# Order of low-weight and high-weight matmuls inside the up projections of two feed-forward layers

## The reference

```
def squared_relu_mlp(hn, w_up, w_down):                       # twice, w_up 1024 x 4096
    return jnp.square(jax.nn.relu(hn @ w_up)) @ w_down
...
hf = _rms_norm(x, norm_ffn_pre[l])                            # once, w_up 1024 x 5632
u = _dwconv_causal(hf @ w_up[l], ffn_dw[l]) + ffn_dw_b[l]
u_g, u_v = jnp.split(u, 2, axis=-1)
yff = (jax.nn.silu(u_g) * u_v) @ w_down[l]
```

## Time and profile before

| | |
|---|---|
| median of 3 runs | 1251.53 us (1250.41 to 1251.58) |
| profiled execution | 1249.54 us |
| its span, first to last instruction | 1247.8 us |
| mean granted TensorE clock | 0.998 |
| PE busy | 1217.6 us, 98% of the span |
| weight loads (PEld) busy | 1095.9 us, 88% |
| DVE busy | 872.1 us, 70% |
| ACT busy | 699.9 us, 56% |
| mean HBM traffic | 168 GB/s |

### The profile page before, as it was taken

One profiled execution on the slowest core, in us unless ns is written; L12 is line 12 of the kernel. 1 busy time (PEld: TensorE's weight loads), 2 busy tenths in 40 slices (PEclk: granted clock), 3 DMA queues, 4 the chain that ended last, 5 costly groups with the idle time before them and its releaser, 6 DMA issues.

```text
span 1247.8 us, 21521 instructions
## 1 busy us (share of the span) xinstructions
PE 1217.6 (98%) x8583; PEld 1095.9 (88%) x8583; DVE 872.1 (70%) x1252; ACT 699.9 (56%) x1016; POOL 58.4 (5%) x102
## 2 busy tenths in 40 slices
PE   8999989999999999999999999999999999999997
PEld 7999978888888998888888999999999977888886
DVE  5898467566666656666656579999656577778876
ACT  5984565555455554555554664666453456666663
POOL 5020020000000001000000000000000010000000
PEclk9999999999999999999999999999999999999999
DMA  7771134666554644465555566354546634566551
GB/s 224 195 203 70 36 126 148 222 207 206 177 186 147 216 164 142 171 204 180 177 193 169 169 203 186 121 161 150 183 148 202 196 108 136 185 199 196 189 193 68
DMA packets 160340, 210.80 MB, mean 169 GB/s; under 512 B 5542, under 2 KB 143220, under 8 KB 160261
## 3 DMA queue, kind: packets, MB, share of 16 engines
q1 hardware_dynamic: 157315, 202.77, 50.9%
q0 software_dynamic: 1904, 6.85, 1.4%
q10 hardware_dynamic: 1042, 0.07, 0.1%
HBM read 208.62 MB, written 1.05 MB: 168 GB/s over the span
## 4 chain that ended last, share of the span: by engine, by line
PE 77%; DVE 11%; ACT 5%; issue 3%; DMA 2%; SPq 1%; POOL 1%; DVEq 0%; POOLq 0%; ACTq 0%
PE bank L372 16%; PE bank L376 16%; PE bank L375 15%; PE bank L457 15%; PE bank L453 7%; DVE wlo L308 4%; ACT whi L300 2%; PE bank L1428 2%; DVE common L2585 1%; DMA raw<-in_dn_w_in 1%; PE bank L1448 1%; ACT common L756 1%; SPq L3391 1%; PE bank L2006 1%; PE bank L2098 1%
## 5 line engine op out<-in xcount | busy, mean ns | idle before, releaser
L308 DVE TENSOR_TENSOR wlo<-raw,whi 128x2048 fp32r<-128x2048 f32 x190 | 434.7, 2290 | 197.8 <-ACT whi L300 197.5
L300 ACT ACTIVATE whi<-raw 128x2048 fp32r<-128x2048 f32 x190 | 363.1, 1912 | 144.5 <-PE bank L372 43.1
L372 PE MATMUL bank<-xparts,whi 128*128 128x256 f32 x912 | 259.7, 285 | 0.4 <-DVE common L2767 0.4
L376 PE MATMUL bank<-xparts,wlo 128*128 128x256 f32 x912 | 255.5, 280 | 0.0
L375 PE MATMUL bank<-xparts,whi 128*128 128x256 f32 x912 | 253.6, 278 | 0.0
L457 PE MATMUL bank<-xparts,whi 128*128 128x512 f32 x832 | 209.2, 393 | 0.0
L372 PEld LDWEIGHTS bank<-xparts,whi 128*128 128x128 f32 x912 | 171.2, 188 | 2.8 <-issue 2.2
L457 PEld LDWEIGHTS bank<-xparts,whi 128*128 128x128 f32 x832 | 148.7, 188 | 27.4
L375 PEld LDWEIGHTS bank<-xparts,whi 128*128 128x128 f32 x912 | 171.5, 188 | 0.7 <-issue 0.5
L376 PEld LDWEIGHTS bank<-xparts,wlo 128*128 128x128 f32 x912 | 171.3, 188 | 0.0
L372 PE MATMUL bank<-whi,hhi 128*128 128x512 f32 x392 | 155.2, 396 | 3.7 <-DVE hlo L1064 1.9
(11 more groups left out here) (391 smaller groups left out, 1679.0 us busy)
## 6 DMA issues: line engine op xcount, KB each, us to landing
raw<-in_mlp_w_up SPq DMA_DIRECT2D x32, 1024.0 KB, 5.5
raw<-in_mlp_w_down SPq DMA_DIRECT2D x32, 1024.0 KB, 5.1
raw<-in_w_in SPq DMA_DIRECT2D x22, 1024.0 KB, 5.2
raw<-in_w_up SPq DMA_DIRECT2D x22, 1024.0 KB, 5.1
raw<-in_w_gate SPq DMA_DIRECT2D x16, 1024.0 KB, 5.5
raw<-in_dn_w_in SPq DMA_DIRECT2D x15, 1024.0 KB, 5.9
raw<-in_mb_w_in SPq DMA_DIRECT2D x12, 1024.0 KB, 5.2
raw<-in_w_down SPq DMA_DIRECT2D x11, 1024.0 KB, 4.9
```

Of the source, the lines that this page charges most:

```text
L300: nc.scalar.activation(whi[:, s, :], raw[:, r, :], ACT.Copy).then_inc(hi_ready, 1)
L308: nc.vector.tensor_tensor(wlo[:, s, :], raw[:, V % RAW, :], f32(whi[:, s, :]), ALU.subtract).then_inc(lo_ready, 1)
L372: ins = pe.matmul(o, shi, mhi, start=first, stop=False, skip_group_check=True)
L376: return pe.matmul(o, slo, mhi, start=False, stop=last, skip_group_check=True)
```

## The change

In the second branch of `wide_features` the second loop over k is taken away, so that the high product of a k follows its low product at once. The matmuls, their operands, their banks, the waits ahead of them and the semaphores that they raise stay the same; only their order inside a feature tile differs.

More of the change, by code:

```diff
@@ L486, in wide_features @@
                             ins.then_inc(unit_begun, 1)
-                    for k in range(KT):
                         ins = high_weights(f, k, k == KT - 1)
```

## The result

The changed kernel is slower by a little: 1255.89 us (median of 6 runs, 1254.85 to 1258.73) against 1251.28 us for the kernel before (6 runs), a ratio of 1.0042 with a 95% interval of 1.0032 to 1.0052 (the ratio is estimated over all runs; the two medians alone give 1.0037). I had forecast no change, 1251.5 us. The time lies inside the range, near its upper end, but outside the 1249.0 to 1254.0 us that I gave to the forecast itself: it went the way of the rival that I called "slower: the long cadence wins". The profiled execution took 1254.85 us with a span of 1253.1 us, 5.3 us longer than before; the clock is the same, 0.998.

A forecast was written before the change was run, and what follows sets the result against it. TensorE's steps, without gaps, were taken to bound the up-unit stages. 800 pairs x 0 ns added 0 us to the median of 1251.5 us, so the forecast was 1251.5 us, with a range of 1247.5 to 1256.4 us.

The forecast's parts named there:

- slower: the long cadence wins: Rival, chance 0.21: in pairs, low steps of 120.0 ns, +3.0 us; with high steps of 236 ns, +6.7 us.
- What bounds the kernel: In up-unit stages time is the sum of TensorE's steps; PE busy all 144.57 us of the first loop.
- The count: 50 up units of 16 pairs move, 800 low and high pairs; 1 ns on a pair is 0.8 us.
- no wait, no idle time: No wait comes or goes in the up units, put at zero; the loop's window should show no idle time.
- What a changed neighbour costs: Inside a tile, changing weights or width costs nothing visible; pairs stay at 116 + 231 ns, 800 x 0 = 0.
- The choice among the bounds: For a pair between 334 and 360 ns, -11 to +10 us, it took the middle, 347.5 ns.
- the short cadence: Low steps of 113.8 ns, as in the second tile; as faster rival, pairs of 340 ns, -6.0 us, chance 0.19.
- its two prices of 231 and 236: High steps in the slower rival's pairs: 231 ns gives +3.0 us in all, 236 ns +6.7 us; chance 0.21.
- my sign for it: In the changed kernel's timeline, an up unit of 5.61 us or more would mean the long cadence.
- What stands before and after a tile meets the same neighbour: At tile ends, still low product first and high product last, so signals come at the same place; put at zero.
- Weight loads two ahead: Low products' loads hiding under high ones: low step 109.2 ns, about -5.7 us; not used in the forecast.

The follow-up runs named there:

- the probe of entries: TensorE-only kernel, equal blocks behind entries of differing width: 256-column steps settled at averages of 118.7, 116.7 or 113.3 ns, pairs at 346.7 or 360.0 ns.
- groups of two: Against the changed kernel, two low products then two high ones through the tile: one run, 1250.50 us beside 1250.12 for before.
- eight and eight at place 0: Kernel before, order kept, with both halves of xparts moved to a multiple of 16 numbers: 1259.14 us, 1.0062 of before.

## Why the prediction was wrong

- *What bounds the kernel* was right. TensorE steps without a gap before and after, and the 4.8 us that the steps grew by are in the span.
- *The count* of 800 pairs was right, and so was *no wait, no idle time*. The loop's window shows none.
- *What a changed neighbour costs* is the step that failed. I read two joins, found them as long as the steps in their blocks, and put the pair at the average of before, 347.5 ns, with 800 x 0 as the sum. A join of before is entered from a settled block and shows one step out of it. It doesn't show the cadence that a run of joins settles into. That is 353 ns here, and the average over an up unit is 351.6 (5.626 / 16 us), 352.5 in the convolutional layer. In place of 0, the 800 pairs cost 3.4 us (2.1 in the low steps, 1.35 in the high ones).
- *The choice among the bounds* was the weak point in it. The rows showed that the same product steps at 113.8 or 118.8 ns, and I took the mean of both, as if a block kept half of its luck. I also took the entries of the two tiles for the same; to the ns they are 236 and 231, and the probe of entries showed that what enters a block can pick its cadence. The low products of the second tile lost the short cadence for good: they average 119.0 now, close to the rival's 120.0; the high ones 233.2, between its two prices of 231 and 236. The direction was that of the slower rival, to which I gave 0.21, and so was the mechanism in the pairs; my sign for it, a unit of 5.61 us or more, is what came. Its price, 3.0 to 6.7 us, holds the pairs' 3.4 and the 4.6 measured, but the down units' 1.35 wasn't in it, and that the whole still fits is luck. That the time lies inside my range is owed to the part of this rival that I took into the range, not to the sum.
- *"What stands before and after a tile meets the same neighbour"*, and so no term for the down units, failed too. The neighbour is the same instruction, but it doesn't hand over in the same time: the last high product ahead of a down unit steps in 227 ns (242.13 to 242.35 above), where it took 236. The untouched 512-column products of the down units hold 238, 231, 231 ns in place of steps that averaged 231.7, 0.041 us a unit and 1.35 us in all, over a quarter of the loss. It depends on the place of the weights that they load: with the hidden tiles at (16, 16) it is gone in the loop.
- *Weight loads two ahead* have no support: pairs would have become faster. In the changed kernel, as before, nearly every load of a low or high product starts 1 to 4 ns after the start of the matmul just ahead of its own.
- What stays open is what in TensorE makes the steps settle. The runs show three things that it depends on (the entry, the order, and the place of an operand in its tile, of the moving one in the probes and of the loaded weights with the hidden tiles) and four that it doesn't depend on here (whether the low product's weights are in `wlo` or `whi`, the half of the bank, other engines, and for 512 columns the width of the load). They don't show the mechanism; that the moment of handing over carries the pattern on fits all of them, but was argued and not measured.

## What to carry to other kernels

Where TensorE runs without gaps, a reordering that keeps every instruction can still move the time by some tenths of a per cent, in either direction (0.4% slower at the kernel's place of `xparts`, some 0.3% faster at the other), and can move it in code behind it that wasn't touched. Don't take the average of an irregular step for the step of a new order: copy the loop's matmuls, with their places in memory, into a kernel that does nothing else, and read the settled steps there; here that gave the loop's units to the nanosecond as long as the tiles had the kernel's sizes too; the convolutional layer, with another order of units, did not follow that copy at (16, 16). Tune order and operand placing together, and compare whole turns of the loop, not the block that was edited.

## What the runs showed that I had not expected

A settled step of an fp32r product took from 112 to 124 ns for 256 columns and from 225 to 241 ns for 512, at a granted clock of 1.00, and repeated in patterns of two to eight steps, or of two turns of a loop (up units of 5.533 and 5.595 us), for as long as the order lasted. Shifting an operand by 12 numbers changed the time of units that don't read it.

The lengths of the settled patterns have a common measure. Averaged over ten turns or more, the loop's turns take 11120.0 ns (before), 11133.4 (groups of two), 11226.6 (changed), 11240.0 (eight and eight at place 0), and 11053.3 and 11146.7 (hidden tiles at (16, 16), eight and eight and then pairs). To within 0.1 ns these are 1668, 1670, 1684, 1686, 1658 and 1672 times 6.667 ns. The pairs of the entry probe, 346.7 and 360.0 ns, are 52 and 54 times that. So a pattern seems to close only on a grid of 6.67 ns; what beats at that rate no run shows.
